# First attention of a two-block transformer kernel: query tiles walked from the last to the first

## The reference

```python
def attend_block(args):          # one block of 128 queries, 8 heads
    qn_b, qr_b, start = args
    s = (jnp.einsum('bqhd,bkhd->bhqk', qn_b, k_nope)
         + jnp.einsum('bqhd,bkd->bhqk', qr_b, k_rope)).astype(jnp.float32) * scale
    q_pos = start + jnp.arange(Q_BLOCK, dtype=jnp.int32)
    causal = k_pos[None, :] <= q_pos[:, None]
    s = jnp.where(causal, s, -jnp.inf)
    p = jax.nn.softmax(s, axis=-1).astype(v.dtype)
    return jnp.einsum('bhqk,bkhd->bqhd', p, v)
```

## Time and profile before

| | us |
|---|---|
| median of 3 runs | 1758.8 |
| lowest, highest | 1753.3, 1763.19 |
| span of the profiled execution | 1747.8 |
| median less that span | 11.0 |
| PE busy in the span | 1647.5 (94%) |
| DVE busy | 932.9 (53%) |
| ACT busy | 576.8 (33%) |
| first scores of the attention to the first `q_exponents` product (536.40 to 633.53) | 97.13 |
| DMA, mean over the span | 83 GB/s |

### The profile page before, as it was taken

The page is one execution under the profiler, slowest core; times in us unless marked ns, Lnnn a source line. Parts: engine busy times, 40 slices in busy tenths (PEclk is TensorE's granted clock), DMA queues, the critical chain, the costliest instruction groups (busy, mean ns, idle before and its releaser), DMA issues.

```text
span 1747.8 us, 30743 instructions
## 1 busy us (share of the span) xinstructions
PE 1647.5 (94%) x12895; PEld 1403.3 (80%) x12895; DVE 932.9 (53%) x1438; ACT 576.8 (33%) x856; POOL 17.9 (1%) x35
## 2 busy tenths in 40 slices
PE   6999999999998998989998999999999899969988
PEld 6999999999986578877777888888878677845767
DVE  3665255655584677654443655434555543536872
ACT  5222122233444441224222322212231454216750
POOL 0000000000000000000000000000000000000000
PEclk9999999999996699999999999999999899968999
DMA  6333334323245000002232222232213412220001
GB/s 239 145 133 98 116 111 144 122 85 120 73 91 92 1 2 3 4 15 73 72 108 96 94 74 96 83 121 81 92 70 107 147 73 80 76 112 1 2 14 59
DMA packets 25957, 145.30 MB, mean 83 GB/s; under 512 B 2720, under 2 KB 2992, under 8 KB 15104
## 3 DMA queue, kind: packets, MB, share of 16 engines
q1 hardware_dynamic: 20768, 123.24, 20.0%
q0 software_dynamic: 5088, 20.58, 4.3%
HBM read 138.58 MB, written 5.23 MB: 82 GB/s over the span
## 4 chain that ended last, share of the span: by engine, by line
PE 82%; DVE 10%; ACT 4%; issue 3%; DMA 1%; DVEq 0%; ACTq 0%; SPq 0%
PE PS L498 21%; PE PS L499 21%; PE PS L500 21%; DVE WLO L1479 2%; PE PS L765 2%; PE PS L775 2%; PE PS L800 1%; ACT WHI L1099 1%; PE PS L692 1%; DVE UMB L1961 1%; PE PS L787 1%; DVE TTT L1990 1%; PE PS L866 1%; PE PS L882 1%; DVE TG L2039 1%
## 5 line engine op out<-in xcount | busy, mean ns | idle before, releaser
L498 PE MATMUL PS<-UH,WHI 128*128 128x264 f32 (+1 forms) x1640 | 547.6, 334 | 28.8 <-DVE WLO L1479 25.4
L499 PE MATMUL PS<-UH,WLO 128*128 128x264 f32 (+1 forms) x1640 | 543.2, 331 | 0.0
L500 PE MATMUL PS<-UL,WHI 128*128 128x264 f32 (+1 forms) x1640 | 541.1, 330 | 0.0
L498 PEld LDWEIGHTS PS<-UH,WHI 128*128 128x128 f32 x1640 | 310.4, 189 | 66.9 <-DVE WLO L1479 18.5
L499 PEld LDWEIGHTS PS<-UH,WLO 128*128 128x128 f32 x1640 | 310.3, 189 | 30.6 <-issue 1.9
L500 PEld LDWEIGHTS PS<-UL,WHI 128*128 128x128 f32 x1640 | 310.2, 189 | 29.9
L1479 DVE TENSOR_TENSOR WLO<-RAW,WHI 128x2048 fp32r<-128x2048 f32 (+3 forms) x125 | 253.5, 2028 | 125.3 <-ACT WHI L1099 124.8
L1099 ACT ACTIVATE WHI<-RAW 128x2048 fp32r<-128x2048 f32 (+3 forms) x125 | 212.0, 1696 | 261.0 <-PE PS L500 248.6
L498 PE MATMUL PS<-GH,WHI 128*128 128x264 f32 (+1 forms) x528 | 169.8, 322 | 4.6 <-DVE GL L1556 2.9
L499 PE MATMUL PS<-GH,WLO 128*128 128x264 f32 (+1 forms) x528 | 169.5, 321 | 0.0
L500 PE MATMUL PS<-GL,WHI 128*128 128x264 f32 (+1 forms) x528 | 169.2, 320 | 0.0
(11 more groups left out here) (372 smaller groups left out, 2252.1 us busy)
## 6 DMA issues: line engine op xcount, KB each, us to landing
RAW<-in_f1u SPq DMA_DIRECT2D x22, 1024.0 KB, 4.8
RAW<-in_f2u SPq DMA_DIRECT2D x22, 1024.0 KB, 4.8
ADA<-in_ada POOLq DMA_DIRECT2D x24, 512.0 KB, 4.8
RAW<-in_f1d SPq DMA_DIRECT2D x16, 704.0 KB, 4.1
RAW<-in_f2d SPq DMA_DIRECT2D x16, 704.0 KB, 4.1
RAW<-in_wi SPq DMA_DIRECT2D x10, 1024.0 KB, 4.8
RAW<-in_w SPq DMA_DIRECT2D x8, 1024.0 KB, 4.8
RAW<-in_mg SPq DMA_DIRECT2D x8, 1024.0 KB, 4.8
```

Source lines behind the costliest of these rows:

```text
L498: mm(out, WHI[:, slot, c:c + w], hi, start=first, stop=False)
L499: mm(out, WLO[:, slot, c:c + w], hi, start=False, stop=False)
L500: return mm(out, WHI[:, slot, c:c + w], lo, start=False, stop=last)
```

## The change

The table LATENT lists the query tiles in the reverse order: 528 keys in steps 0 to 3, then 400, 272 and 144. A new field g counts the tiles as they are worked, and every wait that counts closed tiles goes by g and not by qi. The wait before step 12 is taken out: the widest tile comes before the first product of line 704 now. All side work stays tied to the step's number i.

```diff
-    LATENT = [dict(qi=qi, j=j, w=P * (qi + 1), n=N_META + P * (qi + 1), last=j == 3)
-              for qi in range(QT) for j in range(4)]
+    LATENT = [dict(g=g, qi=QT - 1 - g, j=j, w=P * (QT - g), n=N_META + P * (QT - g), last=j == 3)
+              for g in range(QT) for j in range(4)]
...
-                        if i == 12:
-                            pe.wait_ge(ak_ev, NB)
...
-                    if x["qi"]:
-                        pe.wait_ge(den_rdy, x["qi"])
+                    if x["g"]:
+                        pe.wait_ge(den_rdy, x["g"])
...
-                    g = LATENT[i - 1]["qi"]
+                    g = LATENT[i - 1]["g"]
...
-                    if x["j"] == 0 and x["qi"]:
-                        pe.wait_ge(o_free, x["qi"])
+                    if x["j"] == 0 and x["g"]:
+                        pe.wait_ge(o_free, x["g"])
...
-                    act.wait_ge(ot_f, qi + 1)
+                    act.wait_ge(ot_f, LATENT[i - 3]["g"] + 1)
...
-                    dve.wait_ge(ot_hi, qi + 1)
+                    dve.wait_ge(ot_hi, LATENT[i - 4]["g"] + 1)
...
-                    dve.wait_ge(den_rdy, qi + 1)
+                    dve.wait_ge(den_rdy, g + 1)
                     TT(OTF1[:, :], PS[:, 6, :], DSB1[:, :], ALU.mult).then_inc(o_free, 1)
-                    dve.wait_ge(o_free, qi + 1)
+                    dve.wait_ge(o_free, g + 1)
                     dve.sem_inc(ot_f, 1)
-                    if qi == QT - 1:
+                    if g == QT - 1:
                         q_exponents((4, 5))
```

More of the change, by code:

```diff
@@ L1826, in latent_attention @@
                 if 0 <= i - 2 < n and LATENT[i - 2]["last"]:
-                    qi = LATENT[i - 2]["qi"]
+                    g = LATENT[i - 2]["g"]
                     dve.wait_ge(pv_done, i - 1)
-                    dve.wait_ge(den_rdy, qi + 1)
+                    dve.wait_ge(den_rdy, g + 1)
                     TT(OTF1[:, :], PS[:, 6, :], DSB1[:, :], ALU.mult).then_inc(o_free, 1)
-                    dve.wait_ge(o_free, qi + 1)
+                    dve.wait_ge(o_free, g + 1)
                     dve.sem_inc(ot_f, 1)
-                    if qi == QT - 1:
+                    if g == QT - 1:
                         q_exponents((4, 5))
```

## The result

The change makes the kernel faster. Four runs of the changed kernel had a median of 1741.6 us (1735.4 to 1742.4), four of the kernel before 1759.2 us: a ratio of 0.9894, interval 0.9865 to 0.9922. A second set on another chip gave 0.991 (0.9882 to 0.9939).

The account below looks back on a forecast made before the run. PE, partly at 1.2 GHz, was the bound, with DVE's queue full in steps 0 to 3. Savings of 8.3 and 0.8 us less 4.5 for a clock fall, taken as 4.3: span 1743.5 plus 11.0 gives 1754.5 us (1746 to 1770).

Parts of the forecast that it names:

- the fall of the clock in the last tile: In the 144-key tile, PE's clock falls because little work uses all 128 rows, costing 4.5 us.
- the sum of the five pieces: First scores to first `q_exponents` product, summed by groups of steps: 88.8 us, 8.3 less than 97.13 before.
- the first rival: Clock holds through the 144-key tile: 9.1 us less, 1749.7 us; chance 0.18.
- Steps 0 to 3: 528-key steps beside DVE's side work, DVE's queue the bound: 19.8 us against 14.64 before, bounds 18.4 and 23.
- Step 4: 400-key scores, `per_token` at the low clock and the 528-key tile's close: 16.4 us (13.0 to 17).
- Steps 5 to 7: 400-key steps at 2.4 GHz beside line 704's products: 14.4 us (13.7 to 15).
- Steps 8 to 11: 272-key steps at 2.4 GHz, not shown in the trace of before: 18.5 us (16.3 to 19.2).
- Steps 12 to 15 and the last close: 144-key steps and the close of their tile, before any clock fall: 19.7 us (17 to 21).
- The step from span to median: Whole kernel: the median lies 11.0 us above the profiled span, taking 1743.5 to 1754.5 us.
- The second: Clock falls already in the 272-key steps: 1763 us in full, 1759 taken for a later or shorter fall; chance 0.24.
- The third: Clock falls in steps 1 to 3 and comes back before step 4: 1758.5 us; chance 0.14.
- the fourth: Clock falls in steps 1 to 3 and stays low through the large tiles: 1775 us; chance 0.12.

## Why the prediction was wrong

**What bounds the kernel** was right on both counts. The clock decides most of the stretch: bringing it back at the first close, and nothing else, gives the old order 11.3 of the 16.2 us. DVE's queue decides steps 0 to 3: 2.3 us less on DVE gave 2.0 to 2.1 us. The clock did what the forecast said up to step 11: high through the start, low in `per_token`, back within the first close.

**Two steps failed: the fall of the clock in the last tile**, put at +4.5 us, and the sum of the five pieces, 7.9 us too high. For the first, the clock stayed at 1.00 into line 670 in both profiles of the changed kernel, to 619.6 and 619.2. That step was argued from a count of full-height instructions per step and had no row under it, and the first rival, the one in which the clock holds, got 0.18. In the changed kernel the last tile's steps are also short ones, 2.20 and 2.90 us between the starts of steps 13, 14 and 15. The runs show that it can fall there: with the eight products added at the close it did, and step 12 took 6.69 us and not 5.47; with DVE's 2.3 us moved to step 14 it did too, behind a wait of PE. The three other executions of the changed kernel's first set took 1741.4 to 1742.4 us at a mean clock of 0.970 to 0.972, against 1735.4 us and 0.977 for the profiled one. Whether their clock fell in the last tile or elsewhere is not known.

**The sum** was 88.8 us against 80.9. This is an error of size, and the larger of the two.
- Steps 0 to 3: 19.8 against 19.5, right. DVE is 17.43 us busy.
- Step 4: 16.4 against 14.7. Scores, `per_token` and transposes came out near the forecast (1.82, 7.38, and 1.90 + 0.44 us). The clock was back before the broadcasts ended and not only for step 5: broadcasts 1.36 us in place of 1.99, value products 1.23 in place of 2.5.
- Steps 5 to 7: 14.4 against 13.9, read from a row that showed this very step.
- Steps 8 to 11: 18.5 against 16.9. Three of the four took 3.2 to 4.0 us. The lower bound of 16.3 was near, the middle value was not.
- Steps 12 to 15 and the last close: 19.7 against 15.9. Here 2.9 us are a slip: the 8.98 us of the earlier trace rows begin with the scores of step 15, so "2.9 + 6.0" counted step 15 twice. Without it the piece is 16.8, and the sum 85.9.

From the first scores to the delta rule's first product the forecast had 100.1 us (104.4 - 4.3), and it was 88.0. Of these 12.1 us, 7.9 are the sum; 2.5 the fall inside the stretch; 1.4 line 670's stretch, 7.15 us and not 8.5; the rest is rounding. The remaining kernel took 2.5 us more, not foreseen. Of the signs named ahead, the one on line 670 failed: its first product came at 617.1 and not at 625 to 629 us.

**The step from span to median** was wrong too. The 11.0 us were put down as what lies between an execution's span and the median. In every run here, of both kernels, device time is 1.6 to 1.7 us above the span of its own execution (1735.4 and 1733.7 for the one profiled after). The other 9.3 us have to be that the profiled execution of before was a quick one, by an estimate of 1749.4 us (its span and these 1.6 us): executions of before in the experiments go from 1747.7 to 1767.0 us, with a mean clock of 0.965 at 1748.1 and 0.954 at 1767.0. The profiled execution of after was also the quickest of its four, its median 7.9 us above the span. The span was forecast 9.8 us too high, the median 12.9, so this step put 3.1 us on top.

**The rivals.** The second, a fall in the 272-key steps, didn't come, though those steps can run low: with the small tile ahead of them they did, at 6.7 us each. The third and the fourth need a fall in steps 1 to 3, and PE had 1.00 through all of them. The fourth's condition was tested from the other side: the transposes that were to be without effect raised the clock. With the slip taken out of the sum, the first rival would have stood at 1746.8 and the range's lower end at 1743.1, still above the result: of the 5.0 us that are left in the sum, 1.7 are in step 4, 1.6 in the 272-key and 0.9 in the 144-key steps, both of which the trace of before didn't show at the high clock, and 0.8 elsewhere. The fourth rival's term for steps 5 to 7 is a slip as well: three steps of 8.8 us less 14.4 are 12.0 and not 12.4.

**What the 16.2 us are.** In the old order the return of the clock at the first close makes the stretch 11.3 us shorter: 12.6 behind step 4, less the 1.3 by which the added products lengthen that step. The new order does the same with the transposes and value products that its large tile has anyway, and its stretch is 4.9 us shorter still (80.9 against 85.8). Steps 0 to 3 are 4.9 us longer in it, step 4 is 1.4 shorter, and all behind it takes 46.7 us in place of 55.1; of these 8.4 us the last close with a quarter of the products gives 3.7 (5.31 against 8.98 us). The rest wasn't taken apart. That the clock is the cause of the new order's own time was not tried by holding it low there.

## What to carry to other kernels

This is drawn from one attention. Where PE's clock falls in a part that can't hold it (waits, products with few rows), put the work with the most full-height products right behind that part, so that the clock is back before the long row of steps; what a close is worth isn't its own time but the clock of all that follows. Put the small tiles where nothing of few rows stands beside them. And move side work of a full queue to where that queue is idle, but look whether the place it goes to is already short of PE work: with the same instruction at step 4 the stretch was 3.5 us shorter (77.1 against 80.6, one profile each) than at step 14, where it cost a wait and the clock.

## What the runs showed of the hardware

- A busy PE by itself didn't bring the clock back: it was busy for 20.06 of 20.06 us with the products at the start, and for 26.12 of 26.78 us with the smallest tile second, all at 0.50. Eight full-height products at one place (2.77 us) did, and made their step 1.3 us longer.
- The clock rose behind sixteen added float32 transposes as it did in eight added ordinary products, at 565.1 and 562.8.
- Twelve 8-row products took 0.97 us at the low level with one full-height product between each twelve, and 0.68 us without (108 in 6.09 us).
- Executions of the kernel before on one chip differ by 15 to 19 us in 1750, and the longer ones have the lower mean clock. In one profiled execution the granted clock between 1520 and 1600 us was 0.68 where another kernel's had 0.77, though all instructions behind the attention are the same. A profiled execution may stand at either end, so a forecast built on its span needs a run's own device time beside it, not the median of others.
